# Two fp32r products of specially rounded factors in place of three, in every projection of a two-block transformer kernel

## The reference, cut to what matters

```python
def first_block(x, p, ...):
    h = rms_norm(x, pre_norm_gain)
    q, k, v, z_a, b_gate, c_gate, u, z_c = jnp.split(h @ w_in, 8, axis=-1)
    attn = diff_attention(q, k, v, lam, slopes)          # 4 heads
    attn = rms_norm(attn, subln_gain, SUBLN_EPS) * (1.0 - lambda_init) * silu(z_a)
    conv_out = b_gate * conv3(c_gate * u) * silu(z_c)
    x = x + rms_norm(concat(attn, conv_out) @ w_out, post_norm_gain)
    return x + sigmoid(x @ w_ple_gate) * rms_norm(p @ w_ple_proj, ple_norm_gain)

def second_block(x, meta, ...):                           # 16 meta tokens ahead: 528
    n = rmsnorm(h, norm_mix)
    c_q, c_kv, k_pe, gq, gk, gv, ga, gg, gate_a, gate_b = split(n @ w_in)
    mix = sigmoid(gate_a) * (mla(...) @ w_o_mla) + sigmoid(gate_b) * (gla(...) * silu(gg) @ w_o_gla)
    h = h + mix @ w_out
    return h + peer_ffn(rmsnorm(h, norm_ffn), w_q, sub_keys, u_tab, v_tab)
```

## Time and profile before

| | us |
|---|---|
| median of 3 runs | 2176.52 (2175.61 to 2181.37) |
| span of the profiled execution | 2175.9 |
| PE busy | 2115.4 (97%) |
| DVE busy | 1304.1 (60%) |
| POOL busy | 1033.5 (47%) |
| ACT busy | 922.6 (42%) |
| mean DMA rate | 165 GB/s |

### The profile page before, as it was taken

The page is one execution under the profiler, slowest core; times in us unless marked ns, Lnnn a source line. Parts: engine busy times, 40 slices in busy tenths (PEclk is TensorE's granted clock), DMA queues, the critical chain, the costliest instruction groups (busy, mean ns, idle before and its releaser), DMA issues.

```text
span 2175.9 us, 27394 instructions
## 1 busy us (share of the span) xinstructions
PE 2115.4 (97%) x10296; PEld 1661.6 (76%) x10296; DVE 1304.1 (60%) x2244; ACT 922.6 (42%) x1528; POOL 1033.5 (47%) x892
## 2 busy tenths in 40 slices
PE   8999999999999999999999998999999899999999
PEld 6877767557887776887878877777778788888887
DVE  6456257352235774215898957888881666666664
ACT  4223343572234234111334447777773434343432
POOL 6655546212324122877859887999996100000000
PEclk9999999999999999999999999999999999999999
DMA  5222312201111111233216664777788988888884
GB/s 201 100 78 78 116 61 90 90 30 49 59 40 59 59 55 43 97 122 110 78 59 199 205 206 141 272 289 246 272 291 294 333 300 286 289 284 300 288 287 149
DMA packets 98291, 359.32 MB, mean 165 GB/s; under 512 B 8480, under 2 KB 41504, under 8 KB 73328
## 3 DMA queue, kind: packets, MB, share of 16 engines
q1 hardware_dynamic: 98160, 357.56, 47.3%
HBM read 286.09 MB, written 71.30 MB: 164 GB/s over the span
## 4 chain that ended last, share of the span: by engine, by line
PE 67%; POOL 13%; DVE 11%; issue 6%; ACT 2%; DMA 1%; POOLq 0%; SPq 0%; ACTq 0%; DVEq 0%
PE ps L1438 11%; PE ps L1439 11%; PE ps L802 10%; PE ps L803 9%; PE ps L804 9%; POOL area L2643 6%; POOL wring_parts L2621 6%; PE ps L791 2%; PE ps L1249 2%; DVE area L2413 2%; PE ps L1386 1%; PE ps L1387 1%; DVE area L2410 1%; PE ps L884 1%; PE ps L1225 1%
## 5 line engine op out<-in xcount | busy, mean ns | idle before, releaser
L2577 POOL CAST wring_parts<-wring 128x512 fp32r<-128x512 f32 x236 | 170.5, 764 | 546.0 <-PE ps L804 429.3
L1386 PE MATMUL ps<-sqbuf_parts,wring_parts 128*128 128x512 f32 x1024 | 412.6, 403 | 5.5 <-POOL wring_parts L2621 5.5
L1387 PE MATMUL ps<-normed_x_parts,wring_parts 128*128 128x512 f32 x1024 | 404.4, 395 | 0.0
L2621 POOL TENSOR_TENSOR wring_parts<-wring_parts,wring 128x512 fp32r<-128x512 f32 x256 | 331.0, 1323 | 76.0 <-ACT wring_parts L1856 73.0
L2581 POOL TENSOR_TENSOR wring_parts<-wring,wring_parts 128x512 fp32r<-128x512 f32 x244 | 351.2, 1470 | 6.6 <-ACT wring_parts L1852 1.5
L1386 PEld LDWEIGHTS ps<-sqbuf_parts,wring_parts 128*128 128x128 f32 x1024 | 194.0, 189 | 50.6 <-POOL wring_parts L2621 4.9
L1387 PEld LDWEIGHTS ps<-normed_x_parts,wring_parts 128*128 128x128 f32 x1024 | 193.9, 189 | 41.8
L802 PE MATMUL ps<-resid_parts,wring_parts 128*128 128x512 f32 (+1 forms) x528 | 201.2, 381 | 6.1 <-DVE normed_x_parts L2010 3.3
L803 PE MATMUL ps<-normed_x_parts,wring_parts 128*128 128x512 f32 (+1 forms) x528 | 197.0, 373 | 0.0
L804 PE MATMUL ps<-resid_parts,wring_parts 128*128 128x512 f32 (+1 forms) x528 | 196.2, 372 | 0.0
L1474 ACT ACTIVATE area<-ps 128x1024 f32<-128x1024 f32 (+6 forms) x89 | 61.7, 696 | 275.2 <-PE ps L804 183.5
(11 more groups left out here) (269 smaller groups left out, 4431.4 us busy)
## 6 DMA issues: line engine op xcount, KB each, us to landing
wring<-in_weights_dram SPq DMA_DIRECT2D x65, 1024.0 KB, 4.8
wring<-in_uT_dram SPq DMA_DIRECT2D x128, 512.0 KB, 4.4
area<-in_vT_dram SPq DMA_DIRECT2D x44, 1024.0 KB, 7.2
hidden_table<-area SPq DMA_DIRECT2D x32, 1024.0 KB, 6.7
gate_table<-area SPq DMA_DIRECT2D x32, 1024.0 KB, 8.4
area<-gate_table SPq DMA_DIRECT2D x32, 1024.0 KB, 9.1
wring<-in_vT_dram SPq DMA_DIRECT2D x20, 1024.0 KB, 6.7
rt<-hidden_table SPq DMA_DIRECT2D x32, 512.0 KB, 4.6
```

What stands on the lines that cost most here:

```text
L1386: pe.matmul(out, first[:, d], h_first[:, k, :], start=(k == 0), stop=False)
L1387: mm = pe.matmul(out, rest[:, d], h_rest[:, k, :], start=False, stop=(k == KD - 1))
L2577: ins = nc.gpsimd.tensor_copy(up[:, d, :], W(name)[:, d, :])
L2621: ins = nc.gpsimd.tensor_tensor(rest[:, a:a + PIECE], first[:, a:a + PIECE], u_raw[t % len(USLOT)][:, a:a + PIECE], ALU.subtract)
```

## The change

Every projection now uses the form that the experts' hidden tiles had already: two products, first x first and rest x rest, of factors rounded as told above; `three()` is gone, and so is every L804 matmul. The evacuations multiply by 128, or the gains of the norms do, which DVE multiplies by 128 once at the start. The waits on `weights_split` are per quarter of a tile (a piece of 512 columns of `wring`). `two()`, the waits and one of its callers (the others change alike):

```diff
-            def split_arrived(name):
-                pe.wait_ge(weights_split, SPLIT.index(name) + 1)
-                return W_parts(name)
-            def three(out, a_parts, b_parts, first, last):
-                (a_up, a_low), (b_up, b_low) = a_parts, b_parts
-                pe.matmul(out, a_up, b_up, start=first, stop=False)
-                pe.matmul(out, a_up, b_low, start=False, stop=False)
-                return pe.matmul(out, a_low, b_up, start=False, stop=last)
+            def piece_arrived(name, k):
+                if k in [a for a, _ in low_pieces(name)]:
+                    pe.wait_ge(weights_split, low_count(name, k))
+            def two(out, a_parts, b_parts, first, last):
+                (a_first, a_rest), (b_first, b_rest) = a_parts, b_parts
+                pe.matmul(out, a_first, b_first, start=first, stop=False)
+                return pe.matmul(out, a_rest, b_rest, start=False, stop=last)
...
             def project_parts(key, parts, turn, order=range(KD), first=None):
+                name = f"{key[0]}{key[1]}"
                 claim(key)
-                up, low = split_arrived(f"{key[0]}{key[1]}")
+                up, low = W_parts(name)
                 for m in range(2):
                     d = slice(m * P, (m + 1) * P)
                     for n, k in enumerate(order):
+                        if m == 0:
+                            piece_arrived(name, k)
                         if (key[1] == 0 if first is None else first) and m == 0 and n % 2 == 0:
                             pe.wait_ge(pair_split, 4 * turn + n // 2 + 1)
-                        mm = three(pair(key)[:, m, :], (up[:, k, d], low[:, k, d]),
+                        mm = two(pair(key)[:, m, :], (up[:, k, d], low[:, k, d]),
                                    (parts[0][:, k, :], parts[1][:, k, :]), n == 0, n == KD - 1)
```

The quarters, and the 32 tiles whose firsts ACT makes (before, it made four):

```diff
+def low_pieces(name):
+    _, k, n, _ = WEIGHTS[WN[name]]
+    step = min(k, max(1, PIECE // n))
+    starts = list(range(0, k, step))
+    if name[0:2] == "wo":
+        starts = starts[2:] + starts[:2]
+    return [(a, a + step) for a in starts]
...
+UP_ACT = ["q0", "k0"] + SPLIT[SPLIT.index("wo0"):SPLIT.index("pg3") + 1] + SPLIT[SPLIT.index("gg2"):]
```

ACT's rounding and where it stands in ACT's program (w_in of the tile and the use of the tile two ahead in `SPLIT` are waited for first; one call is two ACTIVATEs of 128x1024):

```diff
+            def round_weights(name):
+                i = SPLIT.index(name)
+                g = WN[name]
+                if i >= NU:
+                    when_filled(act, last_job(SPLIT[i - NU]))
+                act.wait_ge(w_in[g % NW], 16 * (g // NW + 1))
+                pieces = low_pieces(name)
+                for n in (0, 2):
+                    k = slice(pieces[n][0], pieces[n + 1][1])
+                    act.activation(W_parts(name)[0][:, k, :], W(name)[:, k, :], ACT.Copy, scale=GAIN
+                                   ).then_inc(act_rounded, 1)
+            def round_after(name):
+                round_weights(SPLIT[SPLIT.index(name) + NU])
...
+                round_after(f"wo{m}")
                 when_filled(act, ("wo", m))
-                square_two("post", m, pair(("wo", m)))
-                copy_out(("wo", m), mixedT[:, 2 * m:2 * m + 2, :], pair(("wo", m)))
+                square_two("post", m, pair(("wo", m)), scale=float(SCALE))
+                copy_out(("wo", m), mixedT[:, 2 * m:2 * m + 2, :], pair(("wo", m)), scale=float(SCALE))
...
+            round_after("tb0")
             sigmoid(0)
             for m in range(4):
+                round_after(f"ob{m}")
                 if m + 1 < 4:
+                    round_after(f"tb{m + 1}")
                     sigmoid(m + 1)
...
+                round_after(f"w2{m}")
                 when_emptied(act, ("w2", m))
                 square_two("ffn", m, xs[:, 2 * m:2 * m + 2, :])
                 round_gained(2, m, X3_PARTS, x3_gained)
+            round_after("pq0")
             root("ffn", T)
             for m in range(4):
                 round_pair(16 + m, Q_PARTS, 2 * m, hs)
-            act.activation(h_first, hs, ACT.Copy, scale=1.0 / SCALE).then_inc(h_rounded, 1)
+            round_after("pq1")
...
-                if HP - 4 <= h < HP - 2:
-                    name = f"pq{h + 2}"
-                    act.wait_ge(w_in[WN[name] % NW], 16 * (WN[name] // NW + 1))
-                    act.activation(W_parts(name)[0], W(name), ACT.Copy).then_inc(query_up, 1)
+                    if h + NU < HP:
+                        round_after(f"pq{h}")
```

```diff
             def split_pair(n, parts, k, src):
                 dve.wait_ge(pair_rounded, n + 1)
-                dve.tensor_tensor(parts[1][:, k:k + 2, :], src[:, k:k + 2, :], parts[0][:, k:k + 2, :],
-                                  ALU.subtract).then_inc(pair_split, 1)
+                dve.scalar_tensor_tensor(parts[1][:, k:k + 2, :], parts[0][:, k:k + 2, :], float(SCALE - 1),
+                                         src[:, k:k + 2, :], ALU.mult, ALU.subtract).then_inc(pair_split, 1)
...
                 best16(topv, topi_u, sc[:, h], 2 * TT)
-                if h == 0:
-                    dve.wait_ge(h_rounded, 1)
-                    dve.scalar_tensor_tensor(h_rest, h_first, float(SCALE - 1), hs, ALU.mult, ALU.subtract
-                                             ).then_inc(h_split, 1)
-                else:
+                if h:
                     sum_places(h - 1)
```

POOL keeps the rests of all 67 tiles and the firsts of 35 (v0 to za1, cq0 to ta3, gg0 and gg1, of which cq1 to kpe0 and gk0 to gk3 are half as wide), with a `tensor_scalar` of two multiplications in place of the cast, piece by piece; pq6 and pq7 both come after `weigh_places(0)`:

```diff
             def split_group(i):
                 name = SPLIT[i]
                 g = WN[name]
-                _, k, n, _ = WEIGHTS[g]
-                pool.wait_ge(w_in[g % NW], 16 * (g // NW + 1))
-                if i >= NU:
-                    when_filled(pool, last_job(SPLIT[i - NU]))
                 up, low = W_parts(name)
-                step = min(k, max(1, PIECE // n))
-                parts = [slice(a, a + step) for a in range(0, k, step)]
-                if i >= len(SPLIT) - 2:
-                    pool.wait_ge(query_up, i + 3 - len(SPLIT))
-                else:
-                    for d in parts:
-                        ins = nc.gpsimd.tensor_copy(up[:, d, :], W(name)[:, d, :])
-                    ins.then_inc(part_rounded, 1)
-                    pool.wait_ge(part_rounded, i + 1)
-                for d in parts:
-                    ins = nc.gpsimd.tensor_tensor(low[:, d, :], W(name)[:, d, :], up[:, d, :], ALU.subtract)
-                ins.then_inc(weights_split, 1)
...
-            lower_first(0)
-            lower_first(1)
-            for i in range(2, len(SPLIT) - 2):
+                pieces = low_pieces(name)
+                if name not in UP_ACT:
+                    pool.wait_ge(w_in[g % NW], 16 * (g // NW + 1))
+                    if i >= NU:
+                        when_filled(pool, last_job(SPLIT[i - NU]))
+                    before = sum(len(low_pieces(other)) for other in SPLIT[:i] if other not in UP_ACT)
+                def round_piece(n):
+                    k = slice(*pieces[n])
+                    nc.gpsimd.tensor_scalar(up[:, k, :], W(name)[:, k, :], GAIN, 1.0, ALU.mult, ALU.mult
+                                            ).then_inc(part_rounded, 1)
+                if name not in UP_ACT:
+                    round_piece(0)
+                for n, k in enumerate(pieces):
+                    k = slice(*k)
+                    if name in UP_ACT:
+                        pool.wait_ge(act_rounded, act_count(name, n))
+                        if n == 0:
+                            pool.wait_ge(w_first[0] if i == 0 else w_in[g % NW], 16 * (g // NW + 1))
+                        elif i == 0:
+                            pool.wait_ge(w_first[n], 16)
+                    else:
+                        if n + 1 < len(pieces):
+                            round_piece(n + 1)
+                        pool.wait_ge(part_rounded, before + n + 1)
+                    nc.gpsimd.tensor_tensor(low[:, k, :], up[:, k, :], W(name)[:, k, :], ALU.subtract
+                                            ).then_inc(weights_split, 1)
...
                 weigh_places(h)
-                if h < 2:
-                    split_group(len(SPLIT) - 2 + h)
+                if h == 0:
+                    split_group(len(SPLIT) - 2)
+                    split_group(len(SPLIT) - 1)
```

More of the change, by code:

```diff
@@ L925, in first_query @@
                         d = slice(a * P, (a + 1) * P)
-                        mm = three(pair(key)[:, a, :], (up[:, k, d], low[:, k, d]),
+                        mm = two(pair(key)[:, a, :], (up[:, k, d], low[:, k, d]),
                                    (FIRST_PARTS[0][:, k, :], FIRST_PARTS[1][:, k, :]), k == 0, k == KD - 1)
@@ L1604, in _ @@
                     round_pair(1, MIXIN_PARTS, 6, mixin)
+                if u == 13:
+                    round_after("za0")
                 if u == 14:
@@ L1609, in _ @@
             square_heads(1)
+            round_after("za1")
             root("sl1", 1024, "subeps")
@@ L1819, in _ @@
             root("g1", T)
+            round_after("gg0")
             silu(0)
```

164 lines of the change are left out of this document (100 added, 64 removed).

## The result

The changed kernel takes 1989.51 us (median of 4 runs, 1984.59 to 1994.81) against 2178.94 for the kernel before: ratio 0.9131, 95% interval 0.9106 to 0.9155. The forecast was 1995, with 1962 to 2038 around it. The four executions lie in two groups, at 1984.59 and 1985.89 and at 1993.13 and 1994.81 us, and the profiled one is the slowest of them. Its span is 1992.7 us, so span against span 183.2 us went, where the sum had 181; by the medians it is 189.4, and by the spans of the other three executions 184.9 to 193.4.

The account below looks back on a forecast made before the run. PE was taken as the bound, busy 2115.4 of 2175.9 us. Of its 237 us, stage savings came to 187.2, less 6 for the clock, in all 181: 2175.9 - 181 + 0.6 = 1995 us, range 1962 to 2038.

Parts of the forecast that it names:

- PE's 237 us: Whole kernel: removing 1192 matmuls frees 237 us, the most that PE can give.
- pg: Tiles pg0 to pg3: of 14.8 us on PE only 8.2 arrive, since DVE sets the pace at 8.9 us.
- MLA and GLA: 405 to 860 us: 33.9 us saved on gq, gk, gv and 12.4 on ta0 to ta3.
- Up to the ple factor: Start to 302 us, block 1's attention through wo3: savings sum to 62.8 us, with POOL's pacing costing 4.
- cq to kpe: Behind pg, to 405 us: DVE's norm chain doesn't shorten, so only 6.0 us are saved.
- gg to w2 and the late norm factor: 860 us to the ffn: 44.0 and 13.4 us saved; norm factor 7.3 us later, less 3.6, counted as -4.
- The head loop: Up to 1310 us: PE's 29.6 us give nothing; L2435 (4.80) and DVE's wait (4.60) going save 10.5 us.
- The clock, -6: New waits in wo, pg, mix and the ffn: PE restarts at a lower clock, four times 1.4 us lost.
- a granted clock under 0.97 in a stage of projections would make the prediction wrong toward 2050: Sign in any projection stage: a clock below 0.97 would point to a time near 2050 us.
- The rival of POOL's operation: Block 1's attention: POOL becomes the bound if scaling costs what subtraction costs, 22 us more, 2017 us; chance 0.15.
- That of the lower clock at each new wait: Thirty places where tiles meet a wait: the lower clock returns, about 55 us less gain, 2050 us; chance 0.07.
- The fuller gain: Whole kernel: less DVE and POOL disturbance and quarter waits return half of 56 us lost, 1971 us; chance 0.12.

Follow-up runs that it names:

- e6: The changed kernel with a third matmul put back into every projection: 2177.44 us, ratio 0.9991 to the kernel before.
- e5: The changed kernel with a third matmul put back into pg0 to pg3 and pq0 to pq7 alone: 2011.4 us.
- e9: The kernel before, with only POOL splitting seven hidden tiles, not four, ahead of the third `weigh_places`: 2177.13 us against 2176.41.
- e3: The changed kernel with the norm factor of the ffn ahead of the rounding of pq2 on ACT: 1985.97 us.
- e4: The changed kernel with POOL splitting seven hidden tiles, not four, ahead of the third `weigh_places`: 1982.33 us.
- e1: The changed kernel with POOL rounding all weight tiles but q0 and k0, ACT's rounding left out: 2018.07 us.
- e8: The changed kernel with two edits, the ffn's norm factor ahead of pq2's rounding and seven hidden tiles split ahead of the third `weigh_places`: 1977.65 us.

## Why the prediction was right, point by point

- **PE's 237 us, and what is lost of it.** Right. The page shows the 1192 matmuls gone, e6 that without them nothing is gained, and the span lost 183.2 us where the sum had 181. The points of the table lie within 5 us of the forecast up to the head loop. That the sum is met to 2.2 us is in part luck: pg, cq and the head loop gave 11.5 us less than forecast, MLA and GLA 5.7 more (mostly the clock of the profile of before), the -6 of the clock stands in the sum on top of points that were met without it, and the profiled execution is the slowest of four. The sum itself has a slip of 0.4 us: nine tiles of 3.7 less 4 are 29.3 and not 29.7.
- **Up to the ple factor**: 64.4 against 62.8. POOL's pacing in block 1's attention was sized well (41.1 against 41.0).
- **pg.** The mechanism held (e5: 14.8 us of PE's time are worth 3.3 to 3.4), the size didn't: 3.3 us for the term of 8.2. The term took DVE's 8.9 us a tile as fixed, and the steps around the four tiles too. DVE's timeline of the changed kernel:

```profile
251.29 2.19 DVE L2230 TENSOR_TENSOR area<-area 128x1024 f32<-128x1024 f32 x1
253.52 2.20 DVE L2232 TENSOR_TENSOR resid<-resid,area 128x1024 f32<-128x1024 f32 x1
...
260.63 1.92 DVE L2230 TENSOR_TENSOR area<-area 128x1024 f32<-128x1024 f32 x1 [1.58 <-ACT area L1531]
```

  The gate and the sum, 1.22 and 1.52 us at 314.67 before, take 2.19 and 2.20 now, and DVE waits 1.58 us for ACT once: starts lie 9.2 to 9.5 us apart. Beside the gate and the sum POOL had casts before (from 313.62 to 317.93) and has subtractions now (from 247.26 to 254.64). That these are what slows DVE is argued, no run parts them. The normed rows ahead of the first gate also grew, from 5.39 to 7.46 us (DVE L1959 and L2048).
- **cq to kpe**: 4.6 against 6.0, all of it behind DVE's norm chain.
- **MLA and GLA**: 52.0 us against 46.3, and more than the 49.6 us of PE's time that the prediction counted there (34.8 + 14.8). e9, whose code is that of the kernel before up to the head loop, tells why. Its windows in this stage:

```profile
405.00:680.00 275.00, 266.05 (x1384) 196.07 (x1384) 98.16 (x210) 111.24 (x234) 76.67 (x78) 1.00 0.14 51
680.00:860.00 180.00, 174.54 (x819) 123.75 (x819) 118.12 (x159) 67.01 (x117) 47.31 (x42) 1.00 0.15 53
```

  The clock is 1.00 where the earlier trace rows has 0.99, and the stage from the kpe factor to the first GLA factor took 439.9 us in place of 444.8. The profile of before has 10.2 us at the lower level in this stage and e9's has none; at half the speed that is some 5 us, an estimate. About 5 us of the saving are thus the clock in the one profiled execution of before, and without it the term of 46.3 is met (47.1).
- **gg to w2 and the late norm factor.** 47.0 us between the factors of the GLA output and the ffn, where 50.1 were forecast (44.0 + 13.4 - 7.3); the lateness is shown by e3 (7.4).
- **The head loop.** The reasons of this step failed. "PE's 29.6 us for pq0 to pq7 give nothing, because DVE's best-16 chain sets the pace": e5 shows that they do give; with the third matmul back hidden tile 0 begins 22.6 us later against the first best-16 and the gates come 7.6 later. PE's hidden tiles, gapless from the last query on, were the bound together with DVE, and they now begin 22.3 us earlier. What then holds them up is the order on POOL, which the prediction did not look at: tile 4 behind the third `weigh_places` (7.80 us), tile 39 and the exponential behind the last. e4 wins 10.1 us up to the gates. Of the two gains that the step named, L2435 is worth 0.5 to 0.9 us where profiles without a long addition are compared, and not 4.80; and DVE's wait of 4.60 us did go, but for the earlier start of the hidden tiles and not for pq6 and pq7 (8.63 us in e5). The size came out 5.3 us from the first best-16 to the gates in place of 10.5 (251.2 us before, 246.0 now). In e3's profile, with the same code there and no long addition, it is 10.8 (240.4), so that the number can also be met is luck.
- **The clock, -6.** Right in kind: waits of 3.60 and 7.80 us are followed by matmuls 0.42 us apart, and the mean clock went from 0.992 to 0.984. Its cost isn't separable to a microsecond; in pg, where it is low, DVE sets the pace. The sign "a granted clock under 0.97 in a stage of projections would make the prediction wrong toward 2050" came (0.94 and 0.91), and what it stood for didn't: the time came nowhere near 2050.
- **The rival of POOL's operation** is out by the 757 ns; e1 shows that POOL was near enough to the limit for it to matter. That of the lower clock at each new wait is out by the windows (1.00 in gg to w2) and by the time. The fuller gain came only with e8: 1977.65 us.

## What to carry to other kernels

When the busiest engine is relieved by a third, what feeds it must shrink with it: here the sharing of the rounding between two engines (28.6 us) and waits per quarter tile (12.7 us) decided how much of the saving arrived. A loop in which three engines are nearly full has no cover: look up in which order the feeding engine does its other work, since of an early start (22.3 us here) a good part is handed back where an instruction that waits stands ahead of the next piece. Forecast by landmarks of the program rather than by a sum alone, and check each. And when two executions of one kernel differ by 5 us, look for the instruction that differs before an edit of 3 us is judged.

## What the runs showed of the hardware that was not expected

- DVE's small instructions can be held up by POOL's subtractions, of 1.25 us each in an unbroken run: four shifts of 64 columns took 3.88 us against 0.49. One addition of 256 columns took 7.59 us, where two took 2.72; it ended at 1084.06, just behind the end at 1083.78 of a run of eight subtractions, so it took as long as six of them. Other executions of the same code have no such addition (e3). To move an instruction of 5 us ahead of them can cost under 1 us.
- The same code had a lowered clock for some stretches of the MLA and GLA stage in one execution (444.8 us, 10.2 of them at the lower level) and none in another (439.9).
